# Two residual blocks on one core: the table that places projections between attention steps, with query pairs one step sooner

## The reference

```python
h = rms_norm(x, norm_g)
z = h @ w_in.astype(x.dtype)
aq, ak, av, ag, mq, mk, mv, mi, mf, mo, mgate = jnp.split(z, split_points(), axis=-1)
q = rms_norm(aq.reshape(B, L, ATT_HEADS, ATT_HEAD_DIM), q_norm_g)
k = rms_norm(ak.reshape(B, L, ATT_KV_HEADS, ATT_HEAD_DIM), k_norm_g)
q = apply_partial_rope(q, cos, sin)
...
ya = sliding_window_sink_attention(q, k, v, sink).reshape(B, L, ATT_WIDTH)
ya = ya * jax.nn.silu(ag)
qk = jax.nn.silu(causal_depthwise_conv(jnp.concatenate([mq, mk], axis=-1), conv_w, conv_b))
...
hm = mlstm_chunkwise(mq, mk, mv, log_i, log_f)
...
y = jnp.concatenate([ya, ym], axis=-1) @ w_out.astype(x.dtype)
return x + y
```

## Time and profile before

| | |
|---|---|
| median of 3 runs | 2996.37 us (2996.04 to 2997.99) |
| the profiled execution | 2998.21 us, of which the span 2996.4 us |
| TensorE busy | 2900.5 us, 97% |
| VectorE busy | 1630.7 us, 54% |
| ScalarE busy | 1256.1 us, 42% |
| GpSimd busy | 185.8 us, 6% |
| chain that ended last | PE 81%, DVE 10%, ACT 5%, issue 2%, DMA 1% |

### The profile page before, as it was taken

How to read it: one execution, slowest core, us unless ns; L and a number is a source line. 1 busy time by engine, 2 the same in 40 slices (tenths; PEclk the granted TensorE clock), 3 DMA queues, 4 the chain that set the end, 5 groups by cost and what they waited for, 6 DMA issues and landing times.

```text
span 2996.4 us, 42406 instructions
## 1 busy us (share of the span) xinstructions
PE 2900.5 (97%) x17134; PEld 2484.3 (83%) x17134; DVE 1630.7 (54%) x3223; ACT 1256.1 (42%) x2630; POOL 185.8 (6%) x207
## 2 busy tenths in 40 slices
PE   8899999999999999999999999999999999999998
PEld 7888888988887787888888888877898888888886
DVE  6776646367664454676333564335676433564334
ACT  5455423255553243565234333234565324433222
POOL 2100000020000000100000000000100000000000
PEclk9999999999999999999999999999999999999999
DMA  3111221211113222322232222233322232222222
GB/s 117 50 49 58 101 69 64 93 59 52 54 57 108 69 99 92 115 75 72 85 119 85 78 78 85 88 109 99 109 72 80 85 113 90 80 71 92 92 92 84
DMA packets 99726, 250.07 MB, mean 83 GB/s; under 512 B 8597, under 2 KB 44845, under 8 KB 99274
## 3 DMA queue, kind: packets, MB, share of 16 engines
q1 hardware_dynamic: 99530, 247.35, 25.3%
HBM read 239.60 MB, written 6.50 MB: 82 GB/s over the span
## 4 chain that ended last, share of the span: by engine, by line
PE 81%; DVE 10%; ACT 5%; issue 2%; DMA 1%; POOL 1%; SPq 0%; DVEq 0%; POOLq 0%; ACTq 0%
PE ps L93 78%; PE ps L96 3%; ACT Z L99 2%; DVE Z L102 2%; DVE Z L110 2%; DVE cl L102 1%; DMA st<-in_stream_dram 1%; ACT ch L99 1%; DVE ZR L102 1%; DVE Z L106 1%; DVE stat L123 1%; POOL stat L102 1%; DVE stat L110 1%; DVE Z L120 1%; DVE hn L110 0%
## 5 line engine op out<-in xcount | busy, mean ns | idle before, releaser
L93 PE MATMUL ps<-hl,ch 128*128 128x512 f32 (+1 forms) x2512 | 831.0, 359 | 0.0
L93 PE MATMUL ps<-hh,ch 128*128 128x512 f32 (+1 forms) x2368 | 801.6, 365 | 24.1 <-DVE cl L102 9.7
L102 DVE TENSOR_TENSOR cl<-st,ch 128x1024 fp32r<-128x1024 f32 (+1 forms) x436 | 499.9, 1154 | 568.3 <-ACT ch L99 567.1
L93 PE MATMUL ps<-hh,cl 128*128 128x512 f32 (+1 forms) x2368 | 792.2, 361 | 0.0
L99 ACT ACTIVATE ch<-st 128x1024 fp32r<-128x1024 f32 (+1 forms) x436 | 428.7, 990 | 345.6 <-PE ps L93 309.6
L93 PEld LDWEIGHTS ps<-hh,ch 128*128 128x128 f32 x2368 | 422.6, 190 | 106.4 <-ACT Z L99 14.3
L93 PEld LDWEIGHTS ps<-hl,ch 128*128 128x128 f32 x2512 | 448.1, 190 | 72.8
L93 PEld LDWEIGHTS ps<-hh,cl 128*128 128x128 f32 x2368 | 423.1, 190 | 70.7
L99 ACT ACTIVATE Z<-ps 128x512 f32<-128x512 f32 (+7 forms) x506 | 216.1, 436 | 550.8 <-PE ps L93 444.3
L93 PE MATMUL ps<-ZR,ch 128*128 128x512 f32 (+2 forms) x1680 | 437.6, 350 | 2.0 <-DVE cl L102 1.6
L93 PEld LDWEIGHTS ps<-ZR,ch 128*128 128x128 f32 x1680 | 284.5, 189 | 47.6 <-issue 3.9
(11 more groups left out here) (134 smaller groups left out, 3171.7 us busy)
## 6 DMA issues: line engine op xcount, KB each, us to landing
st<-in_stream_dram SPq DMA_DIRECT2D x372, 512.0 KB, 3.4
st<-in_stream_dram SPq DMA_DIRECT2D x64, 256.0 KB, 3.3
Z<-decay_rows SPq DMA_DIRECT2D x8, 904.0 KB, 5.4
Z<-bias_lines SPq DMA_DIRECT2D x16, 448.0 KB, 3.6
ya_spill<-Z SPq DMA_DIRECT2D x8, 512.0 KB, 4.0
Z<-ya_spill SPq DMA_DIRECT2D x2, 2048.0 KB, 7.7
Z<-in_x_dram SPq DMA_DIRECT2D x4, 512.0 KB, 5.3
Z<-in_mem_dram SPq DMA_DIRECT2D x2, 1024.0 KB, 7.0
```

Of the source, the lines that this page charges most:

```text
L93: return Ins(self, self.e and self.e.matmul(o, a, b, start=start, stop=stop, skip_group_check=True))
L102: return Ins(self, self.e and self.e.tensor_tensor(o, a, b, op))
```

## The change

The table puts the first two value products of each column group into one step, directly behind the query pair (and into the first fill), the two convolution tiles into two steps everywhere, and so each query pair one step sooner (3, 11, 19). The gates run in steps 27 to 32, and 33 and 34 have no fill. The meta tokens' attention moves two steps up (`m_s` to 24). The same table serves both layers.

```diff
--- before.py
+++ after.py
@@ -196,19 +196,21 @@
     return out
 def sched1():
 
-    units = [[("mv", c, a) for a in range(5)] + [("cv", 2 * c, 0), ("cv", 2 * c + 1, 0)] for c in range(4)]
+    mv = [[("mv", c, a) for a in range(5)] for c in range(4)]
+    cv = [("cv", t, 0) for t in range(8)]
     ag = [("ag", t, 0) for t in range(8)]
     steps = {s: [] for s in range(-3, 36)}
-    for s in range(-3, 4):
-        steps[s].append(units[0][3 + s])
-    for x, s in enumerate((4, 12, 20)):
+    steps[-3] += mv[0][0:2]
+    for s, task in zip(range(-2, 3), mv[0][2:] + cv[0:2]):
+        steps[s].append(task)
+    for x, s in enumerate((3, 11, 19)):
         steps[s].append(("q", 2 * x + 2, 0))
         steps[s + 1].append(("q", 2 * x + 3, 0))
-        rest = units[x + 1]
-        for y in range(6 if x < 2 else 7):
-            steps[s + 2 + y].append(rest.pop(0))
-        steps[s + 7 if x < 2 else s + 8] += rest
-    for s in range(29, 35):
+        rows = mv[x + 1]
+        steps[s + 2] += rows[0:2]
+        for y, task in enumerate(rows[2:] + cv[2 * x + 2:2 * x + 4]):
+            steps[s + 3 + y].append(task)
+    for s in range(27, 33):
         steps[s].append(ag.pop(0))
     steps[35] = ag
     return steps
@@ -534,11 +536,11 @@
                 put("sB", l, s - 1)
             if 0 <= s - 2 < 32:
                 put("sC", l, s - 2)
+            if l == 0 and s == 24:
+                put("m_s", l)
+            if l == 0 and s == 25:
+                put("m_t", l)
             if l == 0 and s == 26:
-                put("m_s", l)
-            if l == 0 and s == 27:
-                put("m_t", l)
-            if l == 0 and s == 28:
                 put("m_o", l)
             later()
         put("bar", ("att", l))
```

## The result

The changed kernel takes 3005.54 us (median of 10 executions, 3000.44 to 3008.84), the kernel before 2997.40 us (10 executions, 2993.81 to 3000.91). The ratio is 1.0024, with a 95% interval from 1.0016 to 1.0033: slower by 8.1 us, just over what a measurement of this kernel can tell from no change. The profiled execution of the changed kernel has a span of 3004.0 us against 2996.4.

What follows compares the result with a forecast made beforehand. TensorE, busy for 97% of the span, was taken as the bound, so time could only come from its gaps and clock. Terms +1.5 + 6.7 + 2.5 - 1 + 5.0 = +14.7 us gave 3011 us, range 2994 to 3020.

Steps and rivals of the forecast that it cites:

- the forecast's case: The main forecast, slower at 3011 us, with a 53% chance and its own span about 3005 to 3018 us.
- (1): First value step behind each query pair: TensorE waits 0.82 us more for the sums' bank, six places, +4.9 us.
- (3): Middle groups: convolution projections in two steps make VectorE's softmax late, with two waits per group, +6.7 us.
- nothing makes it earlier: Claim behind the pairs: VectorE does the same instructions in the same order, so the bank still comes free at 137.93.
- sign given for (1): In six places TensorE idles 2.2 to 2.9 us ahead of a 128-row value product; wrong if under 1.5.
- (2): Scores reading the new query pair: their wait for its low half goes, -3.4 us in layer 0, nothing in layer 1.
- (4): Stage ends: 1.2 us idle per layer before the last value products, +2.5 us; stage starts nearly a wash, -1 us.
- "worse" rival: Layer starts: ScalarE's standstill moves behind a whole convolution, the query projection waits some 4 us; 3023 us, 12% chance.
- (5): TensorE's clock: three new falls behind idles of about 2 us or more, +5.0 us, between none and +8.4 us.
- The rule that was weighed: Skill page's issue gap, 109 ns against the row's 116 ns per product; would raise the sum by 1.0 us.
- "faster" rival: Waits on ScalarE (5.8 and 8.3 us) vanish everywhere once VectorE's work is spread evenly: -10.1 us, 2986 us, 13% chance.
- "covered" rival: VectorE catches up in the query steps, middle groups cost 0, no new clock falls: +3 us, 2999 us, 22% chance.

Runs made afterwards that it cites:

- run with the pair not moved: Kernel before with only each layer's two middle groups changed (two value products behind the pair, convolution projections in two steps): 3009.2 us, ratio 1.0040.
- middle groups back: Changed kernel with each layer's two middle groups as before (one value product a step, both convolution projections in one): 2998.0 us, ratio 1.0001.
- sums first: Changed kernel with the sums of a pair's second tile recorded ahead of the rotation of its first: 3001.5 us, ratio 1.0013.
- doubled product late: Changed kernel with a group's last two value products together in its sixth step, not two behind the pair: 3006.1 us, ratio 1.0028.
- sums first in the kernel before: Kernel before with the sums of a pair's second tile recorded ahead of the rotation of its first: 3027.9 us, ratio 1.0102.

## Why the prediction was right, and where it was not

The sign, the range and the forecast's case held: slower, 3005.5 us in a range from 2994 to 3020. The median came out 5.5 us under the forecast of 3011. That the idle time agrees so well (+9.7 forecast, +9.8 found) is luck: (1) was 4.3 us too high, and (3), the starts and the third groups, which the forecast put at nothing, made up for it. By its own steps:

(1) *Two value products behind each pair:* forecast +4.9 us, found +0.6 in the table. This is the step that was mis-sized. The row arithmetic (the bank comes free when it did, TensorE arrives 0.8 us sooner) is borne out where the pair isn't moved: +0.67 to +0.72 us at four places. What failed is "nothing makes it earlier". With the pair a step sooner other work lies beside VectorE's, and its two one-column operations ahead of the sums' release ran shorter. The kernel before, then after:

```profile
193.69 1.21 DVE L110 SCALAR_TENSOR_TENSOR stat<-stat,par 128x1 f32<-128x1 f32 x2
...
193.44 1.32 POOL L102 TENSOR_TENSOR Z<-Z,cst 128x528 f32<-128x528 f32 x1
```

```profile
192.22 0.49 DVE L110 SCALAR_TENSOR_TENSOR stat<-stat,par 128x1 f32<-128x1 f32 x2
...
191.27 1.31 POOL L102 TENSOR_TENSOR Z<-Z,cst 128x528 f32<-128x528 f32 x1
```

The same two operations take 1.21 us when GpSimd's product of 528 columns runs across them and 0.49 us when it starts 0.95 us ahead of them and covers only their first 0.36 us. That is 0.7 us at this pair, about the 0.76 us by which this wait (1.65 us) is shorter than the 2.41 us of the run with the pair not moved. It holds at all six places: from the start of these two operations TensorE's wait ends 4.3 to 4.4 us plus their length later, before and after. In sum they take 7.46 us before and 4.06 us after, 3.4 us less; six times 0.7 us less 3.4 leaves 0.8 us, near the 0.6 found. At the first pair of layer 0 they did not get shorter (0.91 and 1.07 us), and there the wait is 2.23 us, as forecast. No run moved GpSimd's product alone, so that it is the cause is read from the rows. Of the sign given for (1), 2.2 to 2.9 us in six places, one place of six has it; none is under 1.5.

(2) *The pair one step sooner:* -3.4 us, found as forecast, but by another cause. The run with the middle groups back has the sooner pair with one value product behind it, and there 1.17 us per group of layer 0 came back, and 0.8 us in layer 1, where there had been none. With two value products but no wait at the bank (sums first) they came back too. So it is the delay of TensorE behind the pair, product and wait together, that lets the others catch up. (1) and (2) are one trade: a second value product costs 0.4 to 0.7 us at the bank and hides about 1.2 us behind it in layer 0, 0.8 us in layer 1.

(3) *Convolution projections in two steps:* forecast +6.7, found +7.9; two waits on ScalarE at each projection and not one. The cause is the one forecast, VectorE's softmax 6 us or more behind its scores; here unit and softmax around the first projection of the group shown above:

```profile
162.60 0.41 PE L93 MATMUL ps<-mskb,idb 128*128 128x272 bf16 x2
...
168.65 0.72 DVE L123 TENSOR_REDUCE stat<-ps 128x2 f32<-128x544 f32 x1
```

Taking the end of the layer as the price worked. In time the middle groups are worth more than all the rest: put back, the changed kernel is level with the kernel before; put in alone, the kernel before is 11.8 us slower. Both edits take the doubled product along; no run split the convolution projections alone. The nearest to it are the runs with the doubled product late and with the middle groups back, 3006.1 and 2998.0 us, which differ mostly in that. Of the 7.6 us that putting it back gained, the granted clock's mean (0.9899 to 0.9916) accounts for 5, and only 1.6 us are idle in the profile. The parts don't add up by themselves: the 4.3 us of busy time in the profile lie in part in the fall at 66 us, which the edit did not touch.

(4) *The ends:* forecast +2.5 and -1, found +2.7 and +0.7. (By the earlier trace rows the low half ends 2.9 us after 336.76 and not 2.8, which changes nothing.) The 4 us wait of the "worse" rival did come, at 109.37 us and at 687.60 us, and was paid for by the 2.2 us that had stood at the same place and by shorter waits elsewhere in the start.

(5) *The clock:* forecast +5.0 with bounds 0 and +8.4; in the profiled execution -2.8 us, outside the bounds, and over the timed executions about nothing (0.9899 against 0.9900). This step was wrong in kind. It took 2.0 us of idle as the point from which the clock falls, out of three idles that did and three that didn't. After the change a wait of 2.23 us (134.79) kept the clock at 1.00, one of 1.97 us (712.79) was followed by a fall, and the fall of layer 1 near 775 us was gone, behind a wait of 1.86 us (776.15): before and after,

```profile
776.00:778.00 2.00, 2.00 (x12) 1.75 (x11) 1.23 (x4) 0.16 (x1) 1.29 (x2) 0.50 0.00 0
```

```profile
776.00:778.00 2.00, 1.85 (x15) 1.85 (x16) 1.22 (x3) 0.00 (x0) 1.83 (x1) 1.00 0.00 0
```

The wait is 0.23 us shorter there. The length of one wait doesn't decide alone: the wait of 2.0 us near 65 us, the same in all kernels, has a fall behind it in the executions of the kernel before and of the changed one and none with the middle groups back. What else decides stays open, and with it whether the two falls of layer 1 went by the change or by chance. Only long waits are sure: in the attention stages of the first block each of 4.0 us or more, in all kernels here, has a fall at it or behind it.

The rule that was weighed (109 ns for a product of 256 columns by the Trainium skill, TensorE: Matmul & The Clock Gate, Back-to-back issue gap, 116 ns by the row) was worth 1 us and lies under the rest. The "faster" rival falls: evenly spread work has more idle time, not less. The "covered" rival falls with the 7.9 us of (3), although the clock's part of it, no new falls, came true.

## What to carry to other kernels

In a kernel like this one, with one engine busy for 97% and its waits at the ends of chains over two others, removing a wait mostly moved it to a later product; count the idle of the whole stage after the edit, not the wait that was attacked. Read TensorE's busy time beside its idle: with the same products, the difference in busy time went with the clock, and it was as large as the effect under study, so idle alone doesn't rank two versions, and neither does one execution. Heavy work of a slower engine stood better in one step where TensorE has two projections to cover it than in two steps with one each, and a step with no projection right behind such work was the dearest of all (5.53 us, against 1.39 us with no such work ahead).

## What the runs showed that was not expected

A kernel with 8.8 us more idle time than the kernel before takes the same time (middle groups back, 104.7 against 95.9 us not busy, busy time 2893.4 against 2900.5 us, ratio 1.0001). The same wait of 2.0 us, at the same place of the same program, was followed by a fall of the clock in one execution and not in another. VectorE's two one-column operations took from 0.35 us, with no product of GpSimd beside them, up to 1.47 us, and set the length of the wait behind a pair. GpSimd took 2.35 us for an operation on 10 columns beside VectorE's product of 528 columns at 137.39 us in the run with the sums first in the kernel before, and 1.95 us for the same operation in that kernel as it was:

```profile
137.95 1.95 POOL L102 TENSOR_TENSOR stat<-stat,par 128x10 f32<-128x10 f32 x1 [4.54 <-DVE stat L106]
```
